# The first conditioning vectors summed by column halves, and the first value product begun on half of h

## The chip, the cores and the metric

One Trainium2 chip, one core. The metric is the device time of one execution in microseconds (us). The kernel before took a median of 2246.25 us over 3 runs (2244.74 to 2246.75). The profiled execution took 2245.24 us, with a span of 2243.5 us from its first to its last recorded instruction.

The engines are named as in the profile: PE (TensorE, matrix products), PEld (its weight loads), DVE (VectorE), ACT (ScalarE), POOL (GpSimd) and SP (SyncE, which only issues DMAs here). ACTq and SPq are the instruction queues of ACT and SP: a DMA issued by ACT is an ACTq row.

## The reference, cut to what matters

```python
def adaln(c, w, b):
    m = jax.nn.silu(c) @ w + b                      # (1, 1024) @ (1024, 3072)
    shift, scale, gate = jnp.split(m, 3, axis=-1)
    return shift[:, None, :], scale[:, None, :], gate[:, None, :]

def mixer_a(h, w_in, ln_g, ln_b, w_s, b_s, w_out):
    u, v, z = jnp.split(h @ w_in, 3, axis=-1)       # (2048, 1024) @ (1024, 6144)
    u = jax.nn.gelu(u)
    v = layer_norm(jax.nn.gelu(v), ln_g, ln_b)
    ...                                             # 128 x 128 causal mixing of v, per chunk and group
    y = u * mixed.reshape(B, S, A_WIDTH) * jax.nn.silu(z)
    return y @ w_out

# layer 0 (layer 1 is windowed attention, behind the same kind of adaln)
shift, scale, gate = adaln(c, a_ada_w[0], a_ada_b[0])
h = rms_norm(x, a_norm[0]) * (1.0 + scale) + shift
x = x + gate * mixer_a(h, ...)
```

There are 2048 tokens of 1024 features, and everything is float32. Before the first product `h @ w_in` can run, the shift and the scale of layer 0 must be there: two vectors of 1024 numbers, each a weighted sum of the 1024 rows of its columns of `a_ada_w`.

## The kernel before, in words

The tokens are worked through in NG = 4 groups of T = 512 (NC = 4 chunks of 128). The 1024 features are KT = 8 tiles of 128. First comes layer 0 for all four groups, then the key and value products and layer 1. A float32 product is done as three matmuls of rounded parts (`split3`, lines 2246 to 2248): each operand is a rounded part (`w_hi`, and `h[:, kt, 0]`) and a rest (`w_lo`, and `h[:, kt, 1]`). ACT rounds a block of weights (`hi`, line 1289), POOL subtracts to get the rest (`lo`, line 1097), each in two halves of 128x1024.

The change touches the prologue alone, that is all that happens until the first product of group 0 is under way. Its parts, in the code of before:

- **The six conditioning pieces.** `ada_sum(piece)` on DVE forms a piece of 1024 columns: acc = sum over kt of `adw[kt]` times a per-partition scalar, eight instructions of 128x1024 (line 1710 the first, line 1712 the other seven). Piece 0 is the shift of layer 0, piece 1 its scale, piece 2 its gate, pieces 3 to 5 are those of layer 1. The rows come from memory in loads of 512 KB (`load_ada`, line 910) into a ring of ADA_RING = 7, so that SP issues load n when DVE has used up load n - 7. Then PE adds over the partitions: `ada_columns` (line 2259, eight small matmuls) for pieces that are wanted as columns, `ada_rows` (line 2266) for the gates. DVE adds the biases (lines 1716 to 1719) and signals `ga_done`.
- **x.** `xs` is one load of 2 MB (line 892). ACT squares and sums it (line 1327), POOL takes the reciprocal root, ACT scales (line 1380), PE transposes (`x_transposes`, line 2278: tiles 0 to 3 ahead, tiles 4 to 7 between the first pieces of unit 0).
- **h.** `h_round(0, kt)` on ACT (line 1359) writes tile kt of h twice, whole into `hfx` (two buffers, in turn) and rounded, and signals `h_hi`; `h_rest(0, kt)` on DVE (line 1737) subtracts and signals `h_lo`. Both wait for what they read, so the tiles run one after the other.
- **The first products.** `v_slab(j)`, j = 0 to 3, is 512 columns of v for the 512 tokens: two units, one on tiles 0 to 3 of h, one on tiles 4 to 7. A unit is 8 pieces (`unit`), a piece 6 matmuls of 128x512. Unit 0 is done by halves (its first 4 pieces take tiles 0 and 1, the last 4 tiles 2 and 3), unit 1 chunk by chunk.
- **What follows slab 0.** PE transposes the mixing matrices (line 2304), then does `ada_rows(2, 6)`, which waits for the whole of `ada_sum(2)` on DVE, and only then slab 1. DVE, behind its last `h_rest`, first waits for four loads that ACT issues, and then starts `ada_sum(2)`:

```python
                    dve.wait_ge(bc_in, 48)      # gate_a, gate_b, sinks
                    dve.wait_ge(bs_in, 16)      # bsh
                    v.tensor_scalar(bsh[:], bsh[:], 0.5, None, ALU.mult)     # line 1919
                    ada_sum(2)
```

These four loads are issued by ACT at lines 1391 to 1395: `bsh`, `gate_a` and `gate_b` of 512 KB each (a row sent to all 128 partitions) and `sinks` of 8 KB.

Each engine works through its own list in the order written; the waits in that list are the only ties between engines. SP's list is `load_ada(0..15)` with `load_x(0)` ahead of load 5, then the weights of units 0 and 1 (line 774), then `load_ada(16..23)` and the weights of unit 2, whose issue stands behind load 23.

Of the kernel before, what the change touches and what calls it, by code (L numbers as in the profile page):

```python
# [8 lines left out]
ALU = mybir.AluOpType  # L9
# [3 lines left out]
P = 128  # L13
D = 1024
SEQ = 2048
WIDTH = 2 * D
KT = D // P
# [347 lines left out]
ROW_C, ROW_AN, ROW_AB, ROW_KVN, ROW_BN, ROW_LNG, ROW_LNB, ROW_BB = 0, 8, 16, 32, 40, 48, 64, 80  # L365
# [3 lines left out]
ADA_RING = 7  # L369
# [11 lines left out]
def yoco_kernel(nc, x, c, positions, a_norm, a_ada_w, a_ada_b, a_w_in, a_ln_g, a_ln_b, a_w_s, a_b_s,  # L381
# [3 lines left out]
    with ctx:  # L385
# [4 lines left out]
        here = [base]  # L390
# [35 lines left out]
        adw = place("adw", y_at, [ADA_RING, D], F32)  # L426
        acc = [place("acc0", y_at + 4 * K * ADA_RING, [D], F32), place("acc1", v_at + 4 * K, [D], F32)]
# [97 lines left out]
        sc = small("sc", KT)  # L525
# [18 lines left out]
        def bank(b, n=512, at=0):  # L544
            return ps[:, 512 * b + at:512 * b + at + n]
# [195 lines left out]
        def _(sp):  # L741
# [127 lines left out]
            def unit(u):  # L869
                if BUFFER[u] == 2:  # L870

                    sp.wait_ge(y_done, at("y_done", group_of(u) - (product_of(u) is not None), 8))
                elif BUFFER[u] == 3:

                    i = group_of(u)
                    sp.wait_ge(piece_done, PIECES_BY[uz_unit(i, 0, 0)])
                    sp.wait_ge(comb_out[0], combs_out(0, 0))
                for hh in range(2):
                    if BEFORE[u] is not None:
                        sp.wait_ge(piece_done, pieces(BEFORE[u], freed(BEFORE[u], hh)))  # L880
                    if u < FIRST_B:
                        a_half(u, hh)
                    else:
                        b_half(u, hh)

            def load_x(n):
                if n >= 1:
                    sp.wait_ge(xt_full, at("xt_full", n - 1, 8))
                    sp.wait_ge(v_gelu, at("v_gelu", n - 1, 16))
                    sp.wait_ge(comb_out[0], combs_out(0, 0))  # L890
                    sp.wait_ge(piece_done, pieces(ao_block(n - 1, 1, 0), 4))
                sp.dma_start(xs[:], x[0, T * n:T * n + T, :].rearrange("(c p) d -> p c d", p=P)).then_inc(x_in, 16)
# [12 lines left out]
            def load_ada(n):  # L905
                piece, kt = n // KT, n % KT
                if n >= ADA_RING:
                    sp.wait_ge(ada_used, n - ADA_RING + 1)
                w = (a_ada_w if piece < 3 else b_ada_w)[0]
                sp.dma_start(adw[:, n % ADA_RING, :], w[P * kt:P * kt + P, D * (piece % 3):D * (piece % 3) + D]) \  # L910
                    .then_inc(ada_in[n % ADA_RING], 16)

            def keep_turned(i, kt):
                m, _ = stage_of(i, kt)
# [21 lines left out]
                    sp.dma_start(zo[n % 2][32 * q:32 * q + 32, :], tt[n % 2][o:o + 32, :]).then_inc(sw_in[n % 2], 16)  # L936

            for n in range(2 * KT):
                if n == 5:
                    load_x(0)  # L940
                load_ada(n)
            unit(0)
            unit(1)

            for i in range(NG):
# [329 lines left out]
        def _(act):  # L1275
# [6 lines left out]
            def hi(u, halves=(0, 1)):  # L1282
                if kept_split(u):
                    return
                p = BUFFER[u]
                for hh in halves:
                    rows_ = slice(2 * hh, 2 * hh + 2)
                    act.wait_ge(raw_in[2 * p + hh], landed(u))
                    s_.activation(whi[p][:, rows_], raw[p][:, rows_], ACT.Copy).then_inc(w_hi, 1)  # L1289
# [63 lines left out]
            def h_round(n, kt):  # L1353
                b = kt % 4 if n else 4 + kt % 4
                act.wait_ge(xt_full, at("xt_full", n, kt + 1))
                if n == 0 and kt >= 2:
                    act.wait_ge(h_lo, kt - 1)
                for dst_ in (hfw[:, kt, :] if n else hfx[:, kt % 2, :], h[:, kt, 0, :]):
                    last = s_.activation(dst_, bank(b), ACT.Identity, bias=sa[:, kt:kt + 1], scale=ga[:, kt:kt + 1])
                last.then_inc(h_hi, 1)  # L1360
# [21 lines left out]

            x_squares(0)
            x_scale(0)
            hi(0)
            act.wait_ge(ga_done, 1)
            for kt in range(4):
                h_round(0, kt)
            hi(1)
            act.dma_start(wsn[:], a_w_s.rearrange("o g t s -> t (o g) s")).then_inc(ws_in, 16)  # L1390
            act.dma_start(bsh[:], a_b_s.rearrange("o g t -> o (g t)").broadcast_to([P, GROUPS * P])) \
                .then_inc(bs_in, 16)
            act.dma_start(gate_a[:], a_ada_b[:, 2 * D:3 * D].broadcast_to([P, D])).then_inc(bc_in, 16)
            act.dma_start(gate_b[:], b_ada_b[:, 2 * D:3 * D].broadcast_to([P, D])).then_inc(bc_in, 16)
            act.dma_start(sinks[:], b_sinks.broadcast_to([P, HEADS])).then_inc(bc_in, 16)
            for kt in range(4, KT):
                h_round(0, kt)

            for i in range(NG):
                if i == 0:  # L1400
# [280 lines left out]
        def _(dve):  # L1681
# [15 lines left out]
            v.tensor_scalar(lngh[:], cols(ROW_LNG, FT), 0.5, None, ALU.mult)  # L1697
            v.tensor_scalar(lnbh[:], cols(ROW_LNB, FT), 0.5, None, ALU.mult)

            def ada_sum(piece):  # L1700
                there = acc[1 if piece == 1 else 0][:]
                for kt in range(KT):
                    n = KT * piece + kt
                    rows_ = adw[:, n % ADA_RING, :]
                    dve.drain()
                    dve.wait_ge(ada_in[n % ADA_RING], 16 * (n // ADA_RING + 1))
                    if kt == 0:
                        if piece >= 2:
                            dve.wait_ge(ada_mm, piece)
                        v.tensor_scalar(there, rows_, sc[:, 0:1], None, ALU.mult).then_inc(ada_used, 1)  # L1710
                    else:
                        v.scalar_tensor_tensor(there, rows_, sc[:, kt:kt + 1], there,  # L1712
                                               ALU.mult, ALU.add).then_inc(ada_used, 1)

            def ada_columns(shift, scale, row_bias, row_norm, g_dst, s_dst, signal=None):
                v.tensor_tensor(s_dst, shift, cols(row_bias, KT), ALU.add)
# [21 lines left out]
                    .then_inc(h_lo, 1)  # L1738

            ada_sum(0)  # L1740
            ada_sum(1)
            dve.wait_ge(ada_mm, 2)
            ada_columns(bank(0, KT, P), bank(0, KT, P + KT), ROW_AB, ROW_AN, ga[:], sa[:], ga_done)
            for kt in range(KT):
                h_rest(0, kt)

            def table(j, m):
# [494 lines left out]
        def _(pe):  # L2242
# [52 lines left out]
            ada_columns(0, 0, P)  # L2295
            for kt in range(4):
                x_transposes(0, kt)
            ada_columns(1, 0, P + KT)

            def spatial_transposes():  # L2300
                pe.wait_ge(pool_mask, 1)
# [51 lines left out]
            for i in range(NG):  # L2353

                def v_slab(j):
                    def bank_free(cnk):
                        if j >= 1:
                            pe.wait_ge(v_gelu, 4 * j + cnk - 3)
                        elif cnk == 0:
                            pe.wait_ge(h_lo, 2)  # L2360

                    def last_x(k):

                        if k < 4:
                            x_transposes(0, 4 + k)
                        if k == 3:
                            pe.wait_ge(h_lo, 4)

                    for ku in range(2):
                        u = v_unit(0, 2 * j + ku)  # L2370
                        if j >= 1 or ku == 1:
                            pe.wait_ge(h_lo, 4 * ku + 4)
                        unit(u, token(u, 0, lambda k: h[:, 4 * ku + k], ku == 0, ku == 1),
                             bank_free if ku == 0 else None, last_x if j == ku == 0 else None)

                def v_blocks(sv):

# [276 lines left out]
```

## Time and profile before

| | us |
|---|---|
| median of 3 runs | 2246.25 |
| profiled execution, its own time | 2245.24 |
| its span | 2243.5 |
| PE busy in the span | 2165.9 (97%) |
| DVE busy | 1433.3 (64%) |
| ACT busy | 1033.1 (46%) |
| POOL busy | 1042.5 (46%) |

The span is what lies between the first and last recorded instruction. A busy PE is not a PE at its peak: back to back, matmuls of 128x512 start 0.23 us apart at the high clock and 0.43 us apart at the low one, and their own durations (0.39 and 0.63 us) overlap. The granted clock is the column PEclk of the window view: 1.00 is full speed (2.4 GHz), 0.50 half (1.2 GHz). PE's first matmul of unit 0 begins at 38.09 us; before it PE has done only small work.

### The profile page before, as it was taken

The numbers are of one execution on the slowest core, as the hardware profiler recorded it, in microseconds if no ns is written. First come the engines' busy times: TensorE is split into PE (matmuls) and PEld (weight loads), VectorE is DVE, ScalarE is ACT, GpSimd is POOL, SyncE is SP. The second block draws the span as 40 slices with busy tenths as digits, with TensorE's granted clock in tenths as the row PEclk, the third lists the DMA queues.
The fourth block names the chain that finished last, engine by engine and source line by source line (L and its number), as shares of the span: only waits on it lengthen the run. The fifth ranks groups of instructions, "written<-read, shape, count | busy, mean of one in ns | idle before, by whom it ended". The sixth has DMA issues, their size and how long they took to land.

```text
span 2243.5 us, 28745 instructions
## 1 busy us (share of the span) xinstructions
PE 2165.9 (97%) x10390; PEld 1808.9 (81%) x10390; DVE 1433.3 (64%) x1815; ACT 1033.1 (46%) x1898; POOL 1042.5 (46%) x636
## 2 busy tenths in 40 slices
PE   4999999999999999999999999998999999999998
PEld 4887778778888778888778888887888888888886
DVE  5966648757487863554975653966676567656753
ACT  4234446534546644445644445434444444434441
POOL 3456785945544765554675554440222232232222
PEclk9999999999999999999999999998999999999999
DMA  9788999785659795567886556988677796786644
GB/s 345 289 302 308 312 321 348 239 297 177 211 182 337 269 325 179 177 212 277 297 299 232 191 197 233 357 319 329 243 270 244 265 330 240 267 336 243 222 182 167
DMA packets 244782, 592.85 MB, mean 264 GB/s; under 512 B 20929, under 2 KB 96801, under 8 KB 244257
## 3 DMA queue, kind: packets, MB, share of 16 engines
q1 hardware_dynamic: 241680, 585.71, 72.7%
q10 hardware_dynamic: 2960, 5.30, 0.7%
q8 instruction: 83, 1.36, 0.2%
q14 instruction: 59, 0.48, 0.1%
HBM read 461.96 MB, written 119.54 MB: 259 GB/s over the span
## 4 chain that ended last, share of the span: by engine, by line
PE 72%; DMA 7%; DVE 6%; POOL 6%; ACT 3%; DVEq 2%; issue 2%; POOLq 1%; SPq 1%; ACTq 0%
PE ps L2246 21%; PE ps L2248 21%; PE ps L2247 21%; POOL w_lo L1097 4%; DMA w_raw<-in_a_w_in 3%; PE ps L2447 2%; DMA w_raw<-a_weights_combined 1%; PE ps L2496 1%; PE ps L2497 1%; POOL cbl L1116 1%; DVE acc L1712 1%; PE ps L2522 1%; DVE yb L1992 1%; ACT w_hi L1289 1%; DMA r<-b_input 1%
## 5 line engine op out<-in xcount | busy, mean ns | idle before, releaser
L1097 POOL TENSOR_TENSOR w_lo<-w_raw,w_hi 128x1024 fp32r<-128x1024 f32 x244 | 652.5, 2692 | 569.0 <-ACT w_hi L1289 568.7
L1289 ACT ACTIVATE w_hi<-w_raw 128x1024 fp32r<-128x1024 f32 x260 | 272.1, 1057 | 409.5 <-DMA w_raw<-in_a_w_in 370.0
L2246 PE MATMUL ps<-h,w_hi 128*128 128x512 f32 x1024 | 403.0, 394 | 8.6 <-POOL w_lo L1097 8.1
L2248 PE MATMUL ps<-h,w_lo 128*128 128x512 f32 x1024 | 398.9, 390 | 0.0
L2247 PE MATMUL ps<-h,w_hi 128*128 128x512 f32 x1024 | 398.7, 389 | 0.0
L1236 POOL TENSOR_SCALAR_AFFINE_SELECT pt<-pt 128x512 fp32r<-128x512 f32 x128 | 82.4, 644 | 392.8 <-ACT pt L1643 339.5
L2246 PEld LDWEIGHTS ps<-h,w_hi 128*128 128x128 f32 x1024 | 192.2, 188 | 53.2 <-POOL w_lo L1097 13.9
L2248 PEld LDWEIGHTS ps<-h,w_lo 128*128 128x128 f32 x1024 | 192.2, 188 | 40.7
L2247 PEld LDWEIGHTS ps<-h,w_hi 128*128 128x128 f32 x1024 | 192.4, 188 | 38.9 <-issue 0.2
L2246 PE MATMUL ps<-r,w_hi 128*128 128x512 f32 x480 | 191.9, 400 | 0.2 <-DMA r<-b_input 0.2
L2248 PE MATMUL ps<-r,w_lo 128*128 128x512 f32 x480 | 187.7, 391 | 0.0
L2247 PE MATMUL ps<-r,w_hi 128*128 128x512 f32 x480 | 187.5, 391 | 0.0
L2246 PE MATMUL ps<-w_hi,yb 128*128 128x512 f32 x448 | 178.2, 398 | 6.4 <-DVE w_lo L2015 2.2
L1970 DVE SCALAR_TENSOR_TENSOR wz<-wz,ps 128x512 f32<-128x512 f32 x64 | 43.8, 688 | 207.8 <-ACT wz L1505 207.8
L2248 PE MATMUL ps<-w_hi,yb 128*128 128x512 f32 x448 | 174.7, 390 | 0.0
L2247 PE MATMUL ps<-w_lo,yb 128*128 128x512 f32 x448 | 174.5, 390 | 0.0
L1992 DVE TENSOR_TENSOR yb<-vy,yb 128x1024 fp32r<-128x1024 f32 x48 | 118.5, 2468 | 42.2 <-ACT yb L1465 38.7
L1245 POOL TENSOR_TENSOR pp<-pp,rden 128x512 f32<-128x512 f32 x64 | 72.1, 1126 | 128.9 <-DVE rden L2219 128.9
L2246 PE MATMUL ps<-w_hi,r 128*128 128x512 f32 (+1 forms) x352 | 125.8, 357 | 4.5 <-DVE x L2131 1.6
L2248 PE MATMUL ps<-w_hi,r 128*128 128x512 f32 (+1 forms) x352 | 123.5, 351 | 0.0
L2247 PE MATMUL ps<-w_lo,r 128*128 128x512 f32 (+1 forms) x352 | 123.4, 351 | 0.0
L1649 ACT ACTIVATE pp<-ps,negm 128x129 f32<-128x129 f32 x256 | 90.7, 367 | 60.8 <-DVE negm L2204 60.7
(266 smaller groups left out, 4630.8 us busy)
## 6 DMA issues: line engine op xcount, KB each, us to landing
w_raw<-in_a_w_in SPq DMA_DIRECT2D x256, 256.0 KB, 3.7
w_hi<-b_weights_split SPq DMA_DIRECT2D x104, 512.0 KB, 4.3
w_lo<-b_weights_split SPq DMA_DIRECT2D x104, 512.0 KB, 5.9
w_raw<-in_a_w_in SPq DMA_DIRECT2D x52, 512.0 KB, 4.7
w_raw<-in_a_w_out SPq DMA_DIRECT2D x48, 512.0 KB, 5.2
w_hi<-v_weights_combined SPq DMA_DIRECT2D x48, 512.0 KB, 4.1
w_lo<-v_weights_combined SPq DMA_DIRECT2D x48, 512.0 KB, 5.7
w_hi<-a_weights_combined SPq DMA_DIRECT2D x32, 512.0 KB, 6.6
```

The costliest lines, as they stand in the source:

```text
L1097: g.tensor_tensor(wlo[p][:, rows_], raw[p][:, rows_], whi[p][:, rows_].bitcast(F32), ALU.subtract).then_inc(w_lo, 1)
L1116: last = g.tensor_tensor(cbl[m][:, rows_], cbr[m][:, rows_], cbh[m][:, rows_].bitcast(F32), ALU.subtract)
L1236: last = g.affine_select(out=pt[:, 2 + m].rearrange("p (h q) -> p h q", h=4), in_=pt[:, m].rearrange("p (h q) -> p h q", h=4), compare_op= ...
L1245: g.tensor_tensor(p4, p4, rden[:, a % 2, :, None].broadcast_to([P, 4, P]), ALU.mult) \
L1289: s_.activation(whi[p][:, rows_], raw[p][:, rows_], ACT.Copy).then_inc(w_hi, 1)
L1649: last = s_.activation(pp[:, a % 2, n, :], ps[:, 2047 + 256 * n + P:2048 + 256 * n + 2 * P], ACT.Exp, bias=negm[:, a % 2, n:n + 1], accum_ ...
L1970: v.scalar_tensor_tensor(wz[:, ft, :], wz[:, ft, :], 1.0, bank(2 + ft), ALU.add, ALU.mult) \
L1992: v.tensor_tensor(there[:, :, 1, :], y_factor(m, q), there[:, :, 0, :].bitcast(F32), ALU.subtract) \
L2246: t_.matmul(dst_, stat[0], mov[0], start=start, stop=False)
L2247: t_.matmul(dst_, stat[0], mov[1], start=False, stop=False)
L2248: return t_.matmul(dst_, stat[1], mov[0], start=False, stop=stop)
L2447: last = t_.matmul(bank(4 + ft, P, P * cnk), vs[:, cnk, P * ft:P * ft + P], wst[:, g, :], start=True, stop=True)
```

## The change

The two first blocks of the conditioning sum are cut otherwise. Before, piece 0 was all 1024 columns of the shift and piece 1 all 1024 of the scale. Now piece 0 is the first 512 columns of both, and piece 1 the last 512 of both, so that the shift and scale of tiles 0 to 3 of h are there after piece 0. On DVE the eight steps of piece 1 are written between and behind the `h_rest` of tiles 0 to 3. PE begins unit 0 on tiles 0 and 1, and does the columns of piece 1 in the middle of unit 0. The x load, the weights of units 0 and 1 and four small loads of ACT change their places in the lists.

```diff
@@ SP: load_ada
-                sp.dma_start(adw[:, n % ADA_RING, :], w[P * kt:P * kt + P, D * (piece % 3):D * (piece % 3) + D]) \
-                    .then_inc(ada_in[n % ADA_RING], 16)
+                if piece < 2:
+                    src = w[P * kt:P * kt + P, 0:2 * D].rearrange("p (s n) -> p s n", s=2)
+                    sp.dma_start(adw[:, n % ADA_RING, :].rearrange("p (s n) -> p s n", s=2),
+                                 src[:, :, 512 * piece:512 * piece + 512]).then_inc(ada_in[n % ADA_RING], 16)
+                else:
+                    ...
@@ SP: order of the first loads
             for n in range(2 * KT):
-                if n == 5:
+                if n == 2:
                     load_x(0)
+                if n == KT:
+                    unit(0)
                 load_ada(n)
-            unit(0)
             unit(1)
@@ ACT
             x_squares(0)
             x_scale(0)
-            hi(0)
+            hi(0, (0,))
             act.wait_ge(ga_done, 1)
-            for kt in range(4):
+            for kt in range(2):
                 h_round(0, kt)
+            hi(0, (1,))
+            for kt in range(2, 4):
+                h_round(0, kt)
+            act.dma_start(wsn[:], a_w_s.rearrange("o g t s -> t (o g) s")).then_inc(ws_in, 16)
             hi(1)
-            act.dma_start(wsn[:], a_w_s.rearrange("o g t s -> t (o g) s")).then_inc(ws_in, 16)
+            act.wait_ge(ga_done, 2)
+            for kt in range(4, KT):
+                h_round(0, kt)
             act.dma_start(bsh[:], ...).then_inc(bs_in, 16)
             act.dma_start(gate_a[:], ...).then_inc(bc_in, 16)
             act.dma_start(gate_b[:], ...).then_inc(bc_in, 16)
             act.dma_start(sinks[:], ...).then_inc(bc_in, 16)
-            for kt in range(4, KT):
-                h_round(0, kt)
@@ DVE (ada_part is one step of the former ada_sum, its code unchanged)
+            def first_columns(piece):
+                here, n = bank((0, 7)[piece], KT, (P, 0)[piece]), KT // 2
+                tiles = slice(n * piece, n * piece + n)
+                dve.wait_ge(ada_mm, piece + 1)
+                v.tensor_tensor(sa[:, tiles], here[:, 0:n], cols(ROW_AB + n * piece, n), ALU.add)
+                v.tensor_tensor(ga[:, tiles], here[:, n:KT], cols(ROW_AB + KT + n * piece, n), ALU.add)
+                dve.drain()
+                v.scalar_tensor_tensor(ga[:, tiles], ga[:, tiles], 1.0, cols(ROW_AN + n * piece, n), ALU.add, ALU.mult) \
+                    .then_inc(ga_done, 1)
+                dve.drain()
             ada_sum(0)
-            ada_sum(1)
-            dve.wait_ge(ada_mm, 2)
-            ada_columns(bank(0, KT, P), bank(0, KT, P + KT), ROW_AB, ROW_AN, ga[:], sa[:], ga_done)
-            for kt in range(KT):
+            first_columns(0)
+            for kt in range(4):
+                ada_part(1, kt)
+                h_rest(0, kt)
+            for kt in range(4, KT):
+                ada_part(1, kt)
+            first_columns(1)
+            for kt in range(4, KT):
                 h_rest(0, kt)
@@ PE
             ada_columns(0, 0, P)
             for kt in range(4):
                 x_transposes(0, kt)
-            ada_columns(1, 0, P + KT)
...
                     def last_x(k):                   # behind piece k of unit 0
-                        if k < 4:
-                            x_transposes(0, 4 + k)
-                        if k == 3:
+                        if k == 0:
+                            x_transposes(0, 4)
+                            x_transposes(0, 5)
+                        elif k == 1:
+                            x_transposes(0, 6)
+                        elif k == 3:
+                            pe.wait_ge(h_hi, 4)
+                            ada_columns(1, 7, 0)
                             pe.wait_ge(h_lo, 4)
+                        elif k == 4:
+                            pe.wait_ge(ga_done, 2)
+                            x_transposes(0, 7)
+                    def half_there(hh):
+                        if j == 0 and ku == 1:
+                            pe.wait_ge(h_lo, 6 + 2 * hh)
                     for ku in range(2):
                         u = v_unit(0, 2 * j + ku)
-                        if j >= 1 or ku == 1:
-                            pe.wait_ge(h_lo, 4 * ku + 4)
                         unit(u, token(u, 0, lambda k: h[:, 4 * ku + k], ku == 0, ku == 1),
-                             bank_free if ku == 0 else None, last_x if j == ku == 0 else None)
+                             bank_free if ku == 0 else None, last_x if j == ku == 0 else None, half_there)
```

## Rows read from the trace of the kernel before

**Rows 1.** The page, busy us, share and count of each engine.

```profile
PE 2165.9 (97%) x10390; PEld 1808.9 (81%) x10390; DVE 1433.3 (64%) x1815; ACT 1033.1 (46%) x1898; POOL 1042.5 (46%) x636
```

**Rows 2.** Timeline of PE, first 70 us: start us, us, [idle before <- releaser].

```profile
20.92 3.54 PE L2259 MATMUL ps<-ones,acc 128*128 128x1 f32 x16 [11.25 <-DVE acc L1712]
...
38.09 0.76 PE L2246 MATMUL ps<-w_hi,h 128*128 128x512 f32 x1 [4.62 <-DVE h L1737]
...
64.57 1.03 PE L2304 MATMUL ps<-ident,wsn 128*128 128x128 f32 x8
66.11 1.98 PE L2266 MATMUL ps<-acc,ones 128*128 128x512 f32 x4 [0.51 <-DVE acc L1712]
```

**Rows 3.** The chain that ended last, first 70 us: start us, us, what.

```profile
31.55 1.93 PE ps L2259 x16
...
37.25 0.70 DVE h L1737
...
59.46 3.26 DVE acc L1712
```

**Rows 4.** Who waited for whom, PE, 60 to 400 us: total, times, longest.

```profile
PE ps L2246 <- POOL w_lo L1097: 8.4, 11, 1.1
PE ps L2266 <- DVE acc L1712: 0.5, 1, 0.5
```

**Rows 5.** Timeline of DVE, first 150 us.

```profile
11.20 9.57 DVE L1712 SCALAR_TENSOR_TENSOR acc<-adw,sc,acc 128x1024 f32<-128x1024 f32 x7
...
50.49 0.69 DVE L1919 TENSOR_SCALAR bsh<-bsh 128x1024 f32<-128x1024 f32 x1
51.33 0.75 DVE L1710 TENSOR_SCALAR acc<-adw,sc 128x1024 f32<-128x1024 f32 x1
```

**Rows 6.** Timeline of ACT and its queue, first 150 us.

```profile
15.52 1.06 ACT L1327 ACTIVATE junk<-xs 128x1024 f32<-128x1024 f32 x1 [8.69 <-DMA xs<-in_x]
...
22.60 4.26 ACT L1380 ACTIVATE xs<-xs,x_rs 128x1024 f32<-128x1024 f32 x4 [2.28 <-POOL x_rs L1150]
...
38.14 0.40 ACTq L1390 DMA_DIRECT2D wsn<-in_a_w_s  x1
...
40.97 0.45 ACTq L1395 DMA_DIRECT2D sinks<-in_b_sinks  x1
```

**Rows 7.** DMA issues, first 80 us: count, KB, median us to landing.

```profile
xs<-in_x SPq DMA_DIRECT2D x1, 2048.0 KB, 12.0
...
bsh<-in_a_b_s ACTq DMA_DIRECT2D x1, 512.0 KB, 8.4
...
sinks<-in_b_sinks ACTq DMA_DIRECT2D x1, 8.0 KB, 9.2
```

**Rows 8.** Instructions on adw, first 90 us, last line: issue to landing.

```profile
DMA to landing us min/median/max: 3.6/7.9/13.5
```

**Rows 9.** Timeline of all engines, 34 to 36 us.

```profile
32.03 4.64 POOL L1097 TENSOR_TENSOR w_lo<-w_raw,w_hi 128x1024 fp32r<-128x1024 f32 x2 [9.53 <-ACT w_hi L1289]
33.83 0.57 DVE L1719 SCALAR_TENSOR_TENSOR ga<-ga,vec 128x8 f32<-128x8 f32 x1
34.44 0.78 ACT L1359 ACTIVATE hfx<-ps,sa,ga 128x512 f32<-128x512 f32 x1 [1.12 <-DVE ga L1719]
...
35.91 1.31 DVE L1737 TENSOR_TENSOR h<-hfx,h 128x512 fp32r<-128x512 f32 x1 [1.51 <-ACT h L1359]
```

**Rows 10.** Timeline of POOL, 58 to 66 us.

```profile
58.34 6.63 POOL L1097 TENSOR_TENSOR w_lo<-w_raw,w_hi 128x1024 fp32r<-128x1024 f32 x2 [10.47 <-ACT w_hi L1289]
```

**Rows 11.** Windows: length, busy of five engines, PEclk, DMA share, GB/s.

```profile
34.00:36.00 2.00, 0.00 (x0) 0.00 (x0) 0.49 (x2) 1.56 (x3) 2.00 (x2) 0.50 1.01 403
...
44.00:46.00 2.00, 2.00 (x12) 1.57 (x11) 0.06 (x1) 1.25 (x2) 2.00 (x1) 1.00 1.09 372
```

**Rows 12.** Timeline of PE, 1520 to 1534 us.

```profile
1526.07 0.80 PE L2246 MATMUL ps<-hb,w_hi 128*128 128x512 f32 x1 [3.17 <-DVE zg L2138]
...
1532.20 0.40 PE L2248 MATMUL ps<-hb,w_lo 128*128 128x512 f32 x1
```

More of the change, by code:

```diff
@@ L909, in load_ada @@
                 w = (a_ada_w if piece < 3 else b_ada_w)[0]
-                sp.dma_start(adw[:, n % ADA_RING, :], w[P * kt:P * kt + P, D * (piece % 3):D * (piece % 3) + D]) \
-                    .then_inc(ada_in[n % ADA_RING], 16)
+                if piece < 2:
[3 more added lines that the diff above has]
+                else:
+                    sp.dma_start(adw[:, n % ADA_RING, :], w[P * kt:P * kt + P, D * (piece % 3):D * (piece % 3) + D]) \
+                        .then_inc(ada_in[n % ADA_RING], 16)
             def keep_turned(i, kt):
@@ L1698, in _, with ada_part @@
             v.tensor_scalar(lnbh[:], cols(ROW_LNB, FT), 0.5, None, ALU.mult)
+            def ada_part(piece, kt):
+                there = acc[1 if piece == 1 else 0][:]
+                n = KT * piece + kt
+                rows_ = adw[:, n % ADA_RING, :]
+                dve.drain()
+                dve.wait_ge(ada_in[n % ADA_RING], 16 * (n // ADA_RING + 1))
+                if kt == 0:
+                    if piece >= 2:
+                        dve.wait_ge(ada_mm, piece)
+                    v.tensor_scalar(there, rows_, sc[:, 0:1], None, ALU.mult).then_inc(ada_used, 1)
+                else:
+                    v.scalar_tensor_tensor(there, rows_, sc[:, kt:kt + 1], there,
+                                           ALU.mult, ALU.add).then_inc(ada_used, 1)
             def ada_sum(piece):
-                there = acc[1 if piece == 1 else 0][:]
                 for kt in range(KT):
[L1703 to L1713, printed above, removed]
+                    ada_part(piece, kt)
+            def first_columns(piece):
[7 more added lines that the diff above has]
+                    .then_inc(ga_done, 1)
+                dve.drain()
             def ada_columns(shift, scale, row_bias, row_norm, g_dst, s_dst, signal=None):
```

## The prediction

> **What bounds the kernel now.** I read the page first. PE is busy for 2165.9 us of a span of 2243.5 [rows 1], so whatever is not PE time is 78 us in all, and over a third of it stands at the start: the first matmul of unit 0 begins at 38.09, released by DVE's `h_rest` [rows 2]. Next I read the timeline of PE. From 38.09 on it hardly stops: unit 1 ends and the mixing matrices are transposed at 64.57, and at 66.11 `ada_rows(2)` begins behind an idle 0.51 us that DVE's sum of piece 2 ended [rows 2]. That wait is short, but it says that at 66 us PE and DVE are level: there is no slack between them, and what delays DVE's piece 2 delays PE. Then the waits behind it: from 60 to 400 us PE waits 8.4 us for POOL's rests in 11 small waits, and 0.5 us for the sum of piece 2 [rows 4]. These waits hang on weights that are loaded when PE frees a buffer, so they move with PE and don't absorb a delay. The change touches only what comes before 66 us, so the question is at what time `ada_rows(2)` and slab 1 can begin.
>
> **The first block and the start of unit 0.** A step of a piece takes DVE 1.37 us (seven took 9.57) [rows 5]. Piece 0 ended at 20.8 before [rows 2]. x now stands behind two loads of 512 KB and not five. It landed at 15.4 (ACT's squares begin at 15.52; 12.0 us from issue to landing) [rows 6, 7]. A load of 512 KB takes 1.3 us at the 403 GB/s of a window in which the memory is busy [rows 11], so x lands 3 x 1.3 = 3.9 us earlier, and loads 2 to 4 stand behind it: load 2 at 13.1 instead of some 8, just ahead of its use, then one each 1.3 us. Piece 0 so ends at 21.3 (+0.5). PE's columns of it take 3.54 [rows 2]: 25.0. Until then DVE now stands idle; before, it went straight into piece 1.
>
> x: ACT squares from 11.9, and the scaling, 7.1 us behind that (15.52 to 22.60) [rows 6], runs from 19.0 to 23.3. Then ACT rounds the first half of unit 0's weights (now loaded behind x and eight loads: 15.4 + 5 x 1.3, near 21) until 24.4, and POOL subtracts it, 2.3 us (two took 4.64) [rows 9]. `first_columns(0)` ends with an operation on two SBUF operands. The same one took 0.57 at 33.83 and ended with the end of POOL's first subtraction (32.03 + 2.32 = 34.35) [rows 9]; so it ends here with POOL's, at 26.8. ACT's first tile takes 1.47 from there to `h_rest` (34.44 to 35.91), each next one 1.34 (35.91 to 37.25) [rows 3, 9], and `h_rest` itself 0.70 [rows 3]: tile 0 is rounded at 28.3, tile 1 at 29.7. DVE does step 0 of piece 1 (27.7), `h_rest` 0 (29.05), step 1 (30.4), `h_rest` 1 (31.15). Unit 0 begins at 31.2, 6.9 us earlier than before.
>
> **The second block.** What unit 0 gains it has to give back if piece 1 isn't there when its first half ends. The first half is 24 matmuls and 12 small transposes, at the low clock at first, some 9 us: until about 40. DVE needs from 26.9 on: eight steps (10.9 us, the first short: 10.4), four `h_rest` (2.8) and 0.7 of waiting for tile 0, together 13.9: 40.8. To this the port comes. In rows: at 59.46 a step of 1.28 took 3.26, beside two subtractions of POOL which took 6.63 together, and 4.64 where DVE did next to nothing [rows 3, 9, 10]. One step per subtraction, each waits for the other: a subtraction costs DVE 2.0 us and POOL 1.0. In before, piece 1 ran with POOL idle (its first subtraction starts at 32.03, piece 1 ended at 31.4) [rows 3, 9]. Now three subtractions fall into it: the second half of unit 0 (rounded at 30.6) and both of unit 1 (33.3 and 34.6, when their loads land). Three times 2.0 is 6.0: 46.8. POOL's mask of `wsn` comes right behind them and costs between 0 and 1.2; I take 0.6. Piece 1 ends at 47.4, against 31.4.
>
> The Trainium skill (SBUF — State Buffer, "SBUF: two separate sides") calls this an exclusive lock: a VectorE operation with two SBUF inputs and a GpSimd operation that reads SBUF exclude each other for a whole instruction. The trace agrees with it in the 3.26 us above. If the two only shared bandwidth, the sum would be shorter by the wait of `first_columns(0)` and part of the 6.0 us.
>
> PE has by then stood idle for some 7 us. In the idle 4.62 us before 38.09 the granted clock was 0.50 (1.2 GHz), and it was 1.00 (2.4 GHz) only from 44 on [rows 2, 11]; after an idle 3.17 us at 1526.07 the matmuls were slow until 1532.20 [rows 12]. So the columns of piece 1 take 3.54 and not 1.93 [rows 2, 3]: 50.9. `first_columns(1)`, 0.7: 51.7. Tiles 4 to 7: the last but one pair by 1.47 + 1.34 + 0.70, `h_rest` 5 ends at 55.2, `h_rest` 7 at 57.9. Before, line 1919 stood right behind `h_rest` 7 at 50.49 [rows 5]. Unit 0's second half (about 6 to 8 us) and unit 1 (11 us) end near 70, against 64.57.
>
> **The four loads that moved.** DVE can start piece 2 only when `bsh`, `gate_a`, `gate_b` and `sinks` have landed. Before, they were issued between 38.14 (`wsn`, ahead of them) and 40.97 [rows 6], sinks landed at 40.97 + 9.2 = 50.2 [rows 6, 7], and DVE's line 1919 began at 50.49: just in time. Now they stand behind all of `h_round`. ACT's queue runs ahead of ACT: `wsn` was issued at 38.14, when the last wait before it (`h_lo` 2, at 37.95) had come [rows 3, 6]. So the issue begins at `h_rest` 5, 55.4. Landing: the four issues take 2.8 us (38.57 to 41.4), the shortest load of 512 KB took 3.6 [rows 8], three of them are 3.9 us of transfer. Below: 2.8 + 2.0 for the small last one, 4.8. Above: `bsh` took 8.4 beside other loads [rows 7], 11 with the rest. The memory has nothing else to do by then, so I take 3.6 + 2 x 1.3 + 0.2 = 6.4: 61.8. Piece 2 begins 0.84 after line 1919 (50.49 to 51.33) [rows 5]: at 62.6, 11.3 us later than before.
>
> **Its end.** From the first step of piece 2 all is as before: load 23 and unit 2's weights are issued behind it, POOL's two subtractions fall into it. `ada_rows(2)` begins 11.3 us later, 77.4, and PE has waited for it since 71, so 6 us. The clock falls again, now on the path: 14 matmuls at 0.43 instead of 0.23 are +2.8 us (1526.07 to 1532.20) [rows 12]. In before there was one such stretch too, at 38.09, which is now hidden; it is within the 11.3. Sum: 11.3 + 2.8 = 14.1, less up to 1 for small waits behind [rows 4]: 13.1. The profiled execution took 2245.2; with 13.1, 2258.3. The median was 1.0 higher: 2259.
>
> Costs at nothing: loads of 2 KB runs instead of 4 KB (unit 0's weights are such runs too); if they were 10% slower, piece 0 would end 1 to 2 us later. The bigger count of small instructions on DVE (three more) is 0.5 us.
>
> **Rivals.**
> (a) The same chain, but with fewer collisions or no fall of the clock: POOL's subtractions in the gaps where DVE waits for ACT, and unit 2 at the high clock. For it: the four `h_rest` leave gaps. Against it: DVE has hardly a gap from 29 on. 14.1 - 2.8 - 4.0 = 7: 2253.
> (b) No collision costs anything, and PE is warm for piece 1's columns: piece 1 ends at 40.8, tile 5 at 46.9, the four loads land at 53.4, line 1919 is 2.9 late and so is `ada_rows(2)`: 2249. For it: each part is possible. Against it: the row at 59.46.
> (c) The other side, and that the change does what its order suggests: unit 0 is 6.9 us earlier, piece 1 is there when the first half ends, and the loads are on DVE before its last `h_rest`. It decides by one point: line 1919 begins before 50.5. Then all of 6.9, or as little as 2, is gained: 2239 to 2244. Against it: 40.8 is the earliest end of piece 1, and even then the loads are late; for it, only that the loads could land faster than any did.
> (d) More is lost: the loads take 10 us as before, or a later engine loses step: 2264 to 2268.
>
> **Numbers.** Forecast 0.52 (2255 to 2263), (a) 0.22, (b) 0.12, (c) 0.07, (d) 0.07. The range reaches to (b): 2249 to 2264. What this kernel's measurement can tell is 0.2%, 4.5 us. Faster by more than that: 0.05, out of (c); within: 0.12, nearly all of (b) and the weak end of (c); slower 0.83.
>
> **What would show it.** Unit 0 begins near 31; a gap of PE of 5 us or more inside unit 0, ended by DVE's piece 1; steps of 3.2 us in piece 1; line 1919 begins near 62 and waits for a DMA; a gap before `ada_rows(2)` and slow matmuls behind it. Wrong if piece 1 ends before 42, or line 1919 begins before 52.

## The result, and the profile after

| | before | changed |
|---|---|---|
| median, us | 2245.49 (4 runs, 2242.52 to 2246.75) | 2260.76 (4 runs, 2257.85 to 2263.73) |
| ratio, 95% interval | | 1.0066 (1.0053 to 1.0078) |
| span of the profiled execution | 2243.5 | 2259.7 |
| `ada_rows(2)` begins | 66.1 | 78.4 |

The change costs 15.3 us, 0.66%. In a second comparison, with other executions of both, it was 11.7 us (1.0049, 1.0035 to 1.0062). The forecast was 2259, 13.1 us slower. One execution differs from the next of the same kernel by more than some of the terms below (31 executions of the kernel before lay between 2242.77 and 2251.47), so small differences between two traces are not read as effects unless a row shows their cause.

The chain of waits of the changed kernel tells the whole prologue (start us, us, what; short rows between are left out). It is to be read beside [rows 3].

```profile
21.82 3.56 PE ps L2289 x16
...
25.71 1.85 DVE ga L1737
...
31.83 3.23 DVE acc L1722
...
37.04 2.81 DVEq L1715
39.94 3.20 DVE acc L1722
43.23 1.94 DVE acc L1722
...
48.07 3.56 PE ps L2289 x16
...
55.82 0.37 ACTq L1404
...
57.18 5.62 DMA sinks<-in_b_sinks
62.83 0.69 DVE bsh L1949
...
71.82 3.19 DVE acc L1722
75.10 3.21 DVE acc L1722
78.36 3.78 PE ps L2296 x4
```

What to see in it: the end of `first_columns(0)` at 25.71, 1.85 us for an operation of 0.16; DVE steps of 1.28 us that become 3.2 at 31.83 and 39.94, an `h_rest` of 0.69 that takes 2.89 from 36.95 on (it stands in DVE's view below; in the chain it is the 2.81 of DVEq), and a step of 1.94 at 43.23, beside POOL's mask of `wsn` (42.20 to 44.09); the columns of piece 1 on PE only at 48.07, and slow; then sinks, issued at 57.18 and 5.62 us under way, with the halving of bsh at 62.83 behind it; then piece 2, with two slow steps at its end (71.82 and 75.10) as in [rows 3], and PE.

PE's own timeline (start us, us, [idle before <- releaser]) has the two stretches in which it stands still once unit 0 has begun, 7.59 and 7.01 us, against one of 0.51 us in [rows 2]. L2276 is the former L2246, L2289 the former L2259, L2296 the former L2266.

```profile
31.89 0.77 PE L2276 MATMUL ps<-w_hi,h 128*128 128x512 f32 x1 [3.21 <-DVE h L1763]
...
48.07 3.54 PE L2289 MATMUL ps<-ones,acc 128*128 128x1 f32 x16 [7.59 <-DVE acc L1722]
...
70.31 1.03 PE L2333 MATMUL ps<-ident,wsn 128*128 128x128 f32 x8
78.36 3.78 PE L2296 MATMUL ps<-acc,ones 128*128 128x512 f32 x4 [7.01 <-DVE acc L1722]
```

Unit 0 begins at 31.89, 6.2 us earlier than in [rows 2], and unit 1 ends at 70.3, 5.7 us later. DVE's view, as [rows 5]; the line that halves bsh is L1949 now, and what it waited for stands in brackets:

```profile
36.95 2.89 DVE L1763 TENSOR_TENSOR h<-hfx,h 128x512 fp32r<-128x512 f32 x1
...
57.66 0.69 DVE L1763 TENSOR_TENSOR h<-hfx,h 128x512 fp32r<-128x512 f32 x1 [0.65 <-ACT h L1366]
62.83 0.69 DVE L1949 TENSOR_SCALAR bsh<-bsh 128x1024 f32<-128x1024 f32 x1 [4.47 <-DMA sinks<-in_b_sinks]
64.09 0.75 DVE L1720 TENSOR_SCALAR acc<-adw,sc 128x1024 f32<-128x1024 f32 x1 [0.57 <-issue]
```

The windows (length, busy of five engines, PEclk, DMA share, GB/s) show the clock: it falls to 0.50 (1.2 GHz) in each of the two stretches. PE ended its work at 40.5 and at 71.3, and the clock fell near 45.4 and near 76. The second time it comes back between 82 and 84.

```profile
44.00:46.00 2.00, 0.00 (x0) 0.00 (x0) 1.91 (x2) 0.00 (x0) 0.10 (x1) 0.85 0.85 258
46.00:48.00 2.00, 0.00 (x0) 0.00 (x0) 1.83 (x2) 0.00 (x0) 0.00 (x0) 0.50 0.69 223
76.00:78.00 2.00, 0.00 (x0) 0.00 (x0) 2.00 (x1) 1.56 (x2) 2.00 (x2) 0.53 1.04 424
...
82.00:84.00 2.00, 2.00 (x8) 1.62 (x7) 1.66 (x2) 0.00 (x0) 0.82 (x1) 0.76 0.86 340
```

Behind the prologue nothing is new up to 400 us. From 60 to 400 us PE waits as in [rows 4], with the one long wait in place of the short one:

```profile
PE ps L2276 <- POOL w_lo L1104: 8.7, 11, 1.1
PE ps L2296 <- DVE acc L1722: 7.0, 1, 7.0
```

### The profile page after: what moved, and what is told of

The parts are those of the page before. It is cut to its first block, busy times and chain, and to the rows that moved or that the text cites. A ratio compares the mean times of both kernels' runs of the same rounds, so it can differ in the third digit from the quotient of the medians.

```text
span 2259.7 us, 28749 instructions
## 1 busy us (share of the span) xinstructions
PE 2170.4 (96%) x10390; PEld 1812.3 (80%) x10390; DVE 1435.8 (64%) x1818; ACT 1033.0 (46%) x1898; POOL 1042.5 (46%) x636
## 4 chain that ended last, share of the span: by engine, by line
PE 71%; DMA 7%; DVE 7%; POOL 6%; ACT 3%; DVEq 2%; issue 1%; POOLq 1%; SPq 1%; ACTq 0%
PE ps L2276 21%; PE ps L2278 21%; PE ps L2277 21%; POOL w_lo L1104 3%; DMA w_raw<-in_a_w_in 3%; PE ps L2488 2%; DVE acc L1722 1%; PE ps L2538 1%; PE ps L2537 1%; DVE yb L2022 1%; POOL cbl L1123 1%; PE ps L2563 1%; DMA r<-b_input 1%; DMA w_raw<-a_weights_combined 1%; ACT w_hi L1296 1%
## 5 line engine op out<-in xcount | busy, mean ns | idle before, releaser
L2276 PE MATMUL ps<-h,w_hi 128*128 128x512 f32 x1024 | 402.9, 393 | 8.9 <-POOL w_lo L1104 8.5
L2276 PEld LDWEIGHTS ps<-h,w_hi 128*128 128x128 f32 x1024 | 192.2, 188 | 52.9 <-POOL w_lo L1104 13.6
L2276 PE MATMUL ps<-r,w_hi 128*128 128x512 f32 x480 | 192.5, 401 | 2.3 <-DMA r<-b_input 2.2
L2276 PE MATMUL ps<-w_hi,yb 128*128 128x512 f32 x448 | 178.7, 399 | 7.3 <-DVE w_lo L2045 2.0
L2276 PE MATMUL ps<-w_hi,r 128*128 128x512 f32 (+1 forms) x352 | 125.8, 357 | 3.7 <-DVE x L2161 1.6
```

The source lines that it names most:

```text
L2276: t_.matmul(dst_, stat[0], mov[0], start=start, stop=False)
```

## The experiments

Each was measured beside executions of the kernel before on the same chip. "Changed" is the kernel after the change. The ratio and its 95% interval are those to the kernel before.

### The four loads, issued early again

```diff
             act.dma_start(wsn[:], ...).then_inc(ws_in, 16)
+            act.dma_start(bsh[:], ...); act.dma_start(gate_a[:], ...)
+            act.dma_start(gate_b[:], ...); act.dma_start(sinks[:], ...)
             hi(1)
             act.wait_ge(ga_done, 2)
             for kt in range(4, KT):
                 h_round(0, kt)
-            ...                                   # the four loads
```

> The changed kernel, but with bsh, gate_a, gate_b and sinks issued right behind wsn, ahead of the rounding of unit 1. My theory (the four late loads cost 4.5 us behind the last h_rest): the line that halves bsh begins right behind h_rest 7 near 58.4 and not at 62.8, ada_rows(2) near 73.9 and not 78.4, and the idle time of PE ahead of it shrinks from 7.0 to some 2.6 us, too short for the clock to fall, which gives 2.8 us more: 7.3 us faster than the changed kernel, 8 slower than the kernel before. Rival 1 (the clock falls all the same): 4.5 faster than changed, 11 slower than before. Rival 2 (the loads were hidden: something else on DVE was late too, or they only push unit 1's weights back): no gain, 15 slower than before.

Measured: 2253.62 us against 2246.52, 1.0027 (1.0017 to 1.0036): 7.1 us slower than before. DVE's timeline of this kernel:

```profile
57.59 0.69 DVE L1763 TENSOR_TENSOR h<-hfx,h 128x512 fp32r<-128x512 f32 x1 [0.65 <-ACT h L1366]
58.20 0.69 DVE L1949 TENSOR_SCALAR bsh<-bsh 128x1024 f32<-128x1024 f32 x1
```

The line follows `h_rest` 7 at once, 4.6 us earlier than in the changed kernel. PE's timeline:

```profile
48.00 3.55 PE L2289 MATMUL ps<-ones,acc 128*128 128x1 f32 x16 [6.83 <-DVE acc L1722]
...
71.00 1.03 PE L2333 MATMUL ps<-ident,wsn 128*128 128x128 f32 x8
73.81 1.98 PE L2296 MATMUL ps<-acc,ones 128*128 128x512 f32 x4 [1.78 <-DVE acc L1722]
```

PE's idle time ahead of `ada_rows(2)` is 1.78 us, and its four matmuls take 1.98: the clock did not fall (the granted clock is 1.00 from 60 to 78 us). So the late loads cost 4.5 us of DVE, and through the longer idle time the fall of the clock. The gain over the changed kernel (7.1 us slower than before, where that one was 11.7 and 15.3 slower) is 4.6 to 8.2 us. That excludes rival 2; PE's rows exclude rival 1.

### POOL kept out of piece 1

```diff
             x_stage(0)
-            lo(0)
+            lo(0, (0,))
+            pool.wait_ge(ada_used, 2 * KT)        # DVE has done piece 1
+            lo(0, (1,))
             lo(1)
```

> The changed kernel, but POOL starts the rest of the second half of unit 0 and of unit 1 only when DVE has done piece 1. My theory (one subtraction costs a step of DVE 2 us, 6.7 us in all in piece 1): no step of piece 1 above 1.3 us, piece 1 ends near 41.2 and not 47.9, its columns take 1.9 us and not 3.5; some of it is given back, since POOL's three subtractions now meet first_columns(1) and h_rest 4 and 5. h_rest 7 ends near 52 and not 58.4: 6 us faster than the changed kernel, 9 slower than before; the loads are still waited for. Rival (the slow steps are slow for another reason, such as memory traffic into the same ring): steps of 3.2 us stay, piece 1 ends at 47 or later, no gain or a loss.

Measured: 2253.25 against 2246.52, 1.0023 (1.0013 to 1.0033): 6.7 us slower than before. DVE:

```profile
42.67 0.16 DVE L1736 TENSOR_TENSOR sa<-ps,vec 128x4 f32<-128x4 f32 x1 [2.10 <-PE ps L2291]
...
42.98 2.36 DVE L1739 SCALAR_TENSOR_TENSOR ga<-ga,vec 128x4 f32<-128x4 f32 x1
...
51.28 0.69 DVE L1765 TENSOR_TENSOR h<-hfx,h 128x512 fp32r<-128x512 f32 x1 [0.81 <-ACT h L1368]
56.95 0.69 DVE L1951 TENSOR_SCALAR bsh<-bsh 128x1024 f32<-128x1024 f32 x1 [4.97 <-DMA sinks<-in_b_sinks]
```

`first_columns(1)` begins at 42.67 and not at 51.65. Of these 9.0 us this execution had 0.65 before (its first columns came at 24.75 and not 25.40), and 1.65 are PE's columns, which took 1.88 us. The other 6.7 are the slow operations of piece 1; in this kernel none took above 1.29 us. Nothing but POOL was moved, so they were POOL's. Some of it is given back as expected: the operation at 42.98 takes 2.36 and not 0.16, since POOL now subtracts there. `h_rest` 7 ends at 52.0 against 58.4, and `ada_rows(2)` begins 5.9 us earlier than in the changed kernel (6 were expected), but behind an even longer idle time, and with the clock fallen:

```profile
72.48 3.78 PE L2298 MATMUL ps<-acc,ones 128*128 128x512 f32 x4 [9.70 <-DVE acc L1724]
```

### Both

> Both edits together. If the two costs add up as I have it: line bsh begins near 52.1, 1.6 us later than in the kernel before (50.5), ada_rows(2) near 67.7. PE ends unit 1 near 61.5 and waits some 5 us, so the clock falls once more in the path: 1.6 + 2.8 = 4.4 us slower than before, or 1.6 slower if it doesn't fall. Rival (what costs is the order of the second block itself, interleaved with h_rest, and neither loads nor POOL): over 10 us slower than before still. That PE began unit 0 6 us earlier is worth nothing in either, since DVE's piece 2 ends as late.

Measured: 2249.08 against 2246.52, 1.0012 (1.0003 to 1.0021): 2.6 us slower than before.

```profile
52.66 0.69 DVE L1951 TENSOR_SCALAR bsh<-bsh 128x1024 f32<-128x1024 f32 x1
```

```profile
41.46 1.92 PE L2291 MATMUL ps<-ones,acc 128*128 128x1 f32 x16 [0.79 <-DVE acc L1724]
...
52.90 0.47 PE L2278 MATMUL ps<-w_hi,h 128*128 128x512 f32 x1 [0.60 <-DVE h L1765]
...
62.52 1.03 PE L2335 MATMUL ps<-ident,wsn 128*128 128x128 f32 x8
68.23 3.78 PE L2298 MATMUL ps<-acc,ones 128*128 128x512 f32 x4 [4.68 <-DVE acc L1724]
```

The line stands at 52.66, 2.2 us later than in the kernel before, and `ada_rows(2)` at 68.23, 2.1 later. The clock did fall (`ada_rows` takes 3.78 us), the case of 4.4 us, which the interval just holds, like that of 1.6. The two costs together make most of the loss: 2.6 us of 11.7 to 15.3 are left. And unit 1 ends at 62.5, 2.1 us earlier than before, without any use: PE then stands for 4.68 us.

### The kernel before, with the late loads alone

```diff
             hi(1)
             act.dma_start(wsn[:], ...).then_inc(ws_in, 16)
+            for kt in range(4, KT):
+                h_round(0, kt)
             act.dma_start(bsh[:], ...)
             ...
-            for kt in range(4, KT):
-                h_round(0, kt)
```

> The kernel before with one part of the change alone: the four loads issued behind all eight h_round. My theory: they are issued when h_rest 5 is done, near 47.1, sinks lands 7.0 us later, near 54.1, and the line that halves bsh begins there and not at 50.5: 3.6 us slower. PE's wait ahead of ada_rows(2) grows from 0.5 to some 4.1 us; if the clock falls in it, 2.8 us are added: 6.4 slower. Rival (with an idle memory the loads land in 3 to 4 us and are hidden): the same time as before.

Measured: 2250.53 against 2246.52, 1.0022 (1.0008 to 1.0035): 4.0 us slower.

```profile
50.44 0.69 DVE L1737 TENSOR_TENSOR h<-hfx,h 128x512 fp32r<-128x512 f32 x1 [0.31 <-ACT h L1359]
55.87 0.69 DVE L1919 TENSOR_SCALAR bsh<-bsh 128x1024 f32<-128x1024 f32 x1 [4.73 <-DMA sinks<-in_b_sinks]
```

```profile
71.42 3.78 PE L2266 MATMUL ps<-acc,ones 128*128 128x512 f32 x4 [5.27 <-DVE acc L1712]
```

The wait for sinks is 4.73 us, as it was 4.47 in the changed kernel. In this execution PE then waited 5.27 us ahead of `ada_rows(2)` and the clock fell, the case of 6.4 us. The median of 4.0 lies nearer to the case without a fall, 3.6, and its interval (1.8 to 7.9 us) holds both; only that this part alone costs something is clear. (The line is at 55.9 and not at 54.1, since in this execution the columns of piece 1 took 3.55 us and not 1.93.)

### Is the early start worth something if PE needn't wait for piece 2?

In all kernels so far PE waits for DVE's piece 2, whatever it gained before. Two kernels take early loads and the late POOL and move `ada_rows(2, 6)` on PE; the second also lets POOL do unit 0 first and hold unit 1 back until `ga_done` 2. A third makes the same move in the kernel before.

```diff
                     v_slab(0)
                     spatial_transposes()
-                    ada_rows(2, 6)
                     v_slab(1)
...
+                    def gate_rows(k):             # behind piece k of unit 2
+                        if k == 3:
+                            ada_rows(2, 6)
```

> Early loads and late POOL, and ada_rows(2, 6) moved on PE from ahead of slab 1 to behind the fourth piece of unit 2. My theory (the early start of unit 0 was worth nothing only because PE then waits for DVE's piece 2 ahead of slab 1): PE ends unit 1 near 61.5, transposes the mixing matrices and goes into unit 2 at once, near 64.5 and not 68.1; piece 2 ends near 68.1, ahead of the fourth piece of unit 2. No idle time above 1 us, no fall of the clock: the third unit ends near 77.2 and not 79.0, some 2 us faster than the kernel before. Rival (slab 1 then waits for the weights of unit 2 or for gelu, or DVE is late for its later sums): the same time as before, or slower.

> As e5, but POOL does the rest of the second half of unit 0 as soon as piece 1 is done, and that of unit 1 only behind first_columns(1). My theory: the operation that ends first_columns(1) no longer waits for POOL (2.36 us in e3, 0.2 to 1 here), PE doesn't stand still inside unit 0's second half, h_rest 7 ends near 51.5 and unit 1 near 60.5: 1 us faster than e5, 3 faster than before. Rival (h_rest 4 to 7 lose to POOL what first_columns(1) gains): as e5.

> The kernel before with ada_rows(2, 6) moved into unit 2 in the same way, and nothing else: a control for e5. PE waited 0.5 us there, so at most 0.5 us faster; DVE gets its gate 5 us later, which costs nothing if its later sums have that much slack. The same time as before in my theory. Rival (the place of ada_rows alone is worth something): over 2 us faster.

Measured, against 2247.93: 2243.71, 0.9985 (0.9976 to 0.9994) for the first; 2243.49, 0.9984 (0.9975 to 0.9992) for the second; 2245.22, 0.9994 (0.9983 to 1.0005), the same time, for the kernel before with the move alone. PE of the first:

```profile
62.82 1.03 PE L2335 MATMUL ps<-ident,wsn 128*128 128x128 f32 x8
64.53 0.47 PE L2278 MATMUL ps<-w_hi,h 128*128 128x512 f32 x1 [0.68 <-ACT vy L1418]
...
70.09 1.88 PE L2298 MATMUL ps<-acc,ones 128*128 128x512 f32 x4
```

From 58 to 85 us no idle time above 0.7 us is left, and unit 2 begins at 64.5. The kernel is 4.2 us faster than the one before, and so 16 to 20 faster than the changed one: it beats both. But how much of this is the early start's? PE of the kernel before with the move alone:

```profile
64.29 0.48 PE L2246 MATMUL ps<-w_hi,h 128*128 128x512 f32 x1
...
69.84 1.88 PE L2266 MATMUL ps<-acc,ones 128*128 128x512 f32 x4
...
87.93 1.88 PE L2310 MATMUL ps<-wst,ones 128*128 128x512 f32 x4
```

It reaches unit 2 at 64.29 and the row sums behind slab 1 at 87.93, where the first kernel reaches them at 64.53 and 88.18. There unit 0 began 5.9 us earlier (32.29 against 38.23), unit 1 ended only 0.7 us earlier (62.82 against 63.50), and the wait of 0.68 us for gelu took that too. (The comparison is good to about 1 us: unit 1 ended 1.07 us earlier in the trace of the kernel with the move alone than in that of the kernel before, though their code is the same up to there.) The medians of the two lie 1.5 us apart, too little to be told from nothing with 11 and 12 executions that scatter over 9 and 11 us. So the question of this section is not answered with yes: that the early start is worth something, even with the move, is not shown.

The second kernel did what it was to do on DVE (0.16 us for the operation), but from there to the end of `h_rest` 7 it took 8.1 us against 6.7, the line that halves bsh then waited 0.79 us for sinks, and PE waited 1.54 us for gelu ahead of unit 2. It gained nothing more: its rival was right.

### The clock

The prediction gave the clock's second fall 2.8 us of the path. Three kernels fill PE's idle time with work that changes nothing: small transposes (first), matmuls of 128x512 (second), these also in the gap inside unit 0 (third). The changed kernel was measured again beside the last two.

```diff
                     v_slab(0)
                     spatial_transposes()
+                    for _ in range(30):
+                        t_.matmul(bank(6), h[:, 0, 0, 0:P], h[:, 0, 0, :], start=True, stop=True)
                     ada_rows(2, 6)
```

> The changed kernel, with 48 more transposes of the mixing matrices (into a bank that is written anew behind them) in the idle 7.0 us ahead of ada_rows(2): they change nothing that is computed. My theory (the fall of the clock costs 2.8 us of the path): the granted clock stays at 1.00 from 70 to 90 us, ada_rows takes 2.0 and not 3.8 us, and the kernel is 2.8 us faster than the changed one, some 12 slower than before. Rival (the slow matmuls were made up for by waits behind them): the same time as the changed kernel, 15 slower than before.

> The changed kernel, with 30 matmuls of 128x512 (tile 0 of h with itself, into a bank that is written anew behind them) in the idle 7.0 us ahead of ada_rows(2), some 6.8 us of them: they change nothing that is computed. In e7 small transposes stood there, and the clock fell at 79.8 all the same, inside ada_rows. My theory (the fall costs 2.8 us of the path): the granted clock stays 1.00 through ada_rows and unit 2, and the kernel is 2.8 us faster than the changed one in the same call. Rival (what the slow matmuls lose is made up for by waits behind them, as e7's time suggests): no difference.

> As e10 (34 matmuls there), and 32 such matmuls also in the idle 7.6 us inside unit 0, ahead of the columns of piece 1. The columns take 1.9 and not 3.54 us, since the clock stays up: everything behind them, h_rest 7 and the four loads too, comes 1.6 us earlier: 4.4 us faster than the changed kernel, 1.6 faster than e10. Rival (the columns are slow after a DVE wait at either clock): as e10.

> The changed kernel itself, for a comparison with e10 and e11 in one call: 15 us slower than before, as measured. Its idle time ahead of ada_rows(2) is 7.0 us and the line that halves bsh begins near 62.8.

Measured: with transposes 2265.05 against 2247.93, 1.0083 (1.0068 to 1.0097). With matmuls 2260.45 against 2247.43, 1.0054 (1.0041 to 1.0066); in both gaps 2262.83, 1.0071 (1.0059 to 1.0083); the changed kernel beside them 2259.14, 1.0049 (1.0035 to 1.0062). Its line that halves bsh began at 62.72 and its idle time ahead of `ada_rows(2)` was 6.79 us, as expected. Not one of the three is faster than the changed kernel, and the first and the third are slower than it (17.1 and 15.4 us slower than before, against 11.7), so on the total time the theory failed and the rival, that nothing is gained, was nearer. The traces say where it went. The matmuls did keep the clock up; PE of the second kernel and of the third:

```profile
48.88 3.54 PE L2289 MATMUL ps<-ones,acc 128*128 128x1 f32 x16 [7.53 <-DVE acc L1722]
...
79.44 1.98 PE L2296 MATMUL ps<-acc,ones 128*128 128x512 f32 x4 [0.41 <-DVE acc L1722]
```

```profile
48.40 1.84 PE L2289 MATMUL ps<-ones,acc 128*128 128x1 f32 x16
...
76.89 1.98 PE L2296 MATMUL ps<-acc,ones 128*128 128x512 f32 x4 [1.12 <-DVE acc L1722]
```

`ada_rows` takes 1.98 us again, and in the third kernel the columns of piece 1 take 1.84 and not 3.54. Five places of PE's timeline, each as its start less its start in the kernel before (us). The last two columns are the kernel with early loads, late POOL and the rows moved, and the kernel before with the rows moved alone:

| start of | before | changed | changed, again | filled, last | filled, both | all three | moved alone |
|---|---|---|---|---|---|---|---|
| `ada_rows(2)` | 66.1 | +12.2 | +12.1 | +13.3 | +10.8 | | |
| row sums behind slab 1 | 89.7 | +14.5 | +14.6 | +13.3 | +10.8 | -1.5 | -1.8 |
| `ada_rows(5)` | 138.6 | +14.5 | +14.6 | +13.3 | +11.4 | -1.5 | -1.8 |
| first transposes of x for group 1 | 409.9 | +14.4 | +15.9 | +15.5 | +16.0 | -1.8 | -1.8 |
| last logits of attention | 2182.9 | +18.1 | +16.2 | +19.0 | +19.5 | -0.5 | +3.9 |

The clock's fall is in the second row: 2.3 to 2.5 us are added between `ada_rows(2)` and the end of slab 1 in the changed kernel, none in the filled ones. The third kernel is then 3.8 us ahead of the changed one. By 410 us it has lost all of it, in small waits of PE for POOL's and DVE's rests of weights, like these of the third kernel:

```profile
302.40 0.50 PE L2276 MATMUL ps<-h,w_hi 128*128 128x512 f32 x1 [1.05 <-POOL w_lo L1104]
...
340.86 0.50 PE L2276 MATMUL ps<-h,w_hi 128*128 128x512 f32 x1 [1.51 <-POOL w_lo L1104]
```

From 138 to 425 us such waits for POOL add up to 11.0 us in the third kernel, 9.0 and 9.5 in the two executions of the changed one, and 8.6 in the kernel before; those for DVE add 2.1 us more in the third. Why they are longer there was not tried. What follows: the fall costs 2.4 us where it happens, but of a gain of 1 to 4 us at 140 us nothing need be left at 410. The last row is no measure of a change: the kernel with the move alone stood 1.8 us ahead at 410 and 3.9 behind at 2183, though its code is that of the kernel before from there on.

## Why the prediction was right

| step | predicted | measured |
|---|---|---|
| piece 0 ends | 21.3 | 21.7 |
| `first_columns(0)` ends | 26.8 | 27.5 |
| unit 0 begins | 31.2 | 31.9 |
| piece 1 ends | 47.4 | 47.9 |
| columns of piece 1 end | 50.9 | 51.6 |
| `h_rest` 7 ends | 57.9 | 58.4 |
| the four loads issued / landed | 55.4 / 61.8 | 55.8 / 62.8 |
| piece 2 begins | 62.6 | 64.1 |
| `ada_rows(2)` begins | 77.4 | 78.4 |

**The first block.** Right within 0.7 us, and so was the cause of the wait in `first_columns(0)`: its last operation took 1.84 us beside POOL's first subtraction. Most of the 0.7 is POOL's: its reciprocal root took 2.06 us and not 1.53, and ACT was that much later. The Trainium skill (SBUF — State Buffer, "SBUF: two separate sides") has the one that comes second blocked until the whole instruction of the other has ended. The trace agrees: the operation ended at 27.55, POOL's subtraction at 25.18 + 2.35 = 27.53. One slip of the sum was small: squares at 15.52, 3.9 us earlier, are at 11.6 and not 11.9 (12.2 measured). The loads in runs of 2 KB, put at nothing, cost at most the 0.4 us by which piece 0 ended late.

**The second block.** The sum put 6.6 us on POOL, three collisions and the mask of `wsn`; the four held-up operations of the chain cost 1.95, 2.2, 1.9 and 0.65, 6.7 together. One of the three collisions hit an `h_rest` and not a step. With POOL kept away no operation of piece 1 was held up, which shows the cause.

**The loads.** Right in kind, short by 1 us: from the first issue (55.8) to the landing of sinks (issued at 57.2, 5.6 us under way) it was 7.0 us where 6.4 was assumed, and the issue began 0.4 us late. Piece 2 then began 1.26 us behind the line that halves bsh and not 0.84. Of the 1.5 us that this made, 0.5 came back: the sum of piece 2 took 14.3 us to `ada_rows(2)`, 14.8 in the kernel before. Undoing this part and doing it alone both show a wait of 4.5 to 4.7 us on DVE. It is the part of the change that has nothing to do with its idea.

**The step that was mis-sized** is the clock, with what follows it. It was given 2.8 us from the 14 slow matmuls of [rows 12], about 6.1 us at the low clock; here PE ran slowly from 78.4 to about 83, and 2.3 to 2.5 us were lost. The 14.1 us before the last term so became 14.5 at the row sums: 1.0 more ahead of `ada_rows(2)` and 0.4 less behind it, two errors that partly cancel. The last term, "less up to 1 for small waits behind", had no row that showed it, and none does now: at 410 us the changed kernel is 14.4 and 15.9 us late. What comes later can't judge it. Between 139 and 2183 us the changed and the filled kernels of the table lost another 1.6 to 8.1 us, the one with all three edits 1.0 and the kernel before with the move alone 5.7, and the one with early loads won back 1.3 (+7.7 to +6.4). That the total, +15.3 and +11.7 in two comparisons, lies on both sides of the 13.1 forecast is as much as it can say; that it comes so near is in part luck.

**Rivals.** (a), fewer collisions or no fall, does not hold: all collisions came, and the clock fell. (b) had the line that halves bsh 2.9 us late if no collision cost anything; the kernel with POOL out of piece 1 had it 6.5 late (56.95) and lost 6.7 in all, since POOL's work came later, onto `first_columns(1)` and the `h_rest` behind it, and the clock still fell in the path. (c) missed its point by 12.3 us: the line began at 62.8, not before 50.5. (d) does not hold either: from the first issue the loads took 7.0 us, not 10. The nearest to (c) is the kernel with early loads, late POOL and the move of `ada_rows`, and what of its 4.2 us is the early start's is not shown.

## What to carry to other kernels

An engine that is started earlier gains only up to the next thing it must wait for; ask first for the last wait of the stage (here DVE's sum of piece 2), and whether the change brings that one nearer. When a step is moved behind a wait, everything written behind it in the same list moves too: four loads of another stage, in ACT's list, cost 4.0 us alone in the kernel before and 4.6 to 8.2 in the changed one, where the fall of the clock hung on them too. When work on DVE is moved, it meets other work of POOL: each long subtraction of POOL in piece 1 held one operation of DVE up by 1.9 to 2.2 us. Count these meetings before the order is written. And when a new version combines several edits, give each its own control: here, in its trace, the move of `ada_rows` alone brought PE as far as the move with the early start.

## What was not expected of the hardware

- Small transposes in the idle time kept the granted clock at 1.00 while they ran, until 76.9 us in the first filled kernel. PE then idled 2.05 us, and the clock fell at 79.6, inside `ada_rows`; an idle time of 1.78 us behind full matmuls and eight transposes, in the kernel with early loads, left it at 1.00.
- After PE ended at 71.3, the clock of the changed kernel stayed at 1.00 until about 76, 4.8 us. In the kernel before, after PE's work ended at 33.5, it was at 0.50 within 0.3 us [rows 11].
- The first sixteen small matmuls took 3.54 us with a granted clock of 1.00 in the record, and 1.93 ten microseconds later [rows 2, 3]: here the recorded clock and the speed of PE did not agree. In the execution of the kernel before with the late loads alone this lasted longer: the record says 1.00 from 31 to 47 us, but the same columns took 3.55 us at 31.22, and the matmuls from 40.05 on began 0.43 us apart.
